# Reshaping the phase-F weight chunks of a hybrid RetNet / Mamba-2 layer: 8 k-blocks x 256 columns become 4 k-blocks x 512 columns

## What is computed

```
o_ret = (yr * silu(g_ret)) @ w_ret_o          # yr already times ret_gn_w; 2048 x 1024 weights
o_ssd = (ys_normed * ssd_norm_w) @ w_ssd_o    # 2048 x 1024 weights
g_r, g_s = split(gates)                       # gates = h @ w_in[:, 12352:14400]
out = (sigmoid(g_r) * o_ret + sigmoid(g_s) * o_ssd) @ w_out
x_new = x + gate * rmsnorm(out, norm_post)
```

## Time and profile before

| what | us |
|---|---|
| median of the two timed runs | 4121.48 |
| the two timed runs | 4078.60 and 4164.37 |
| the profiled execution | 4029.62 |
| its span on the slowest core, core 6 | 4027.9 |
| spans of the eight cores in it | 4001.4 to 4027.9 |

### The profile page before, as it was taken

One profiled execution on the slowest core, in us unless ns is written; L12 is line 12 of the kernel. 1 busy time (PEld: TensorE's weight loads), 2 busy tenths in 40 slices (PEclk: granted clock), 3 DMA queues, 4 the chain that ended last, 5 costly groups with the idle time before them and its releaser, 6 DMA issues.

```text
span 4027.9 us, 49014 instructions; the slowest of 8 cores (4001.4 to 4027.9 us)
## 1 busy us (share of the span) xinstructions
PE 2515.2 (62%) x15552; PEld 1579.3 (39%) x15552; DVE 1737.8 (43%) x2966; ACT 1341.8 (33%) x3063; POOL 515.8 (13%) x526
## 2 busy tenths in 40 slices
PE   7358679688688536556366363663646635394974
PEld 7335354263263325334153251532524424142431
DVE  0432524415425365564654646656466465010111
ACT  0233242341331325344263352543525435111121
POOL 0020120111201011010110111101101011303213
PEclk9579899899899757767577686776867767697997
DMA  4320110210200100101001000010000000414113
GB/s 134 105 76 17 52 56 6 65 38 11 80 11 17 54 6 6 37 1 33 10 1 42 1 26 17 1 43 1 22 21 1 27 1 28 150 63 146 63 56 133
DMA packets 143692, 166.85 MB, mean 41 GB/s; under 512 B 5072, under 2 KB 128464, under 8 KB 143312
## 3 DMA queue, kind: packets, MB, share of 16 engines
q1 hardware_dynamic: 138960, 146.94, 11.9%
q0 software_dynamic: 4480, 16.78, 1.1%
HBM read 138.54 MB, written 25.17 MB: 41 GB/s over the span
## 4 chain that ended last, share of the span: by engine, by line
PE 43%; DVE 24%; ACT 12%; issue 10%; DMA 5%; POOL 3%; DVEq 1%; ACTq 0%; SPq 0%; POOLq 0%
DVE s_acc L776 8%; PE ps_all L617 7%; PE ps_all L505 6%; PE ps_all L1047 6%; ACT s_Dec L913 5%; PE ps_all L899 4%; PE ps_all L741 3%; PE ps_all L600 3%; DVE s_S L858 3%; PE ps_all L1054 3%; PE ps_all L439 2%; PE ps_all L288 2%; PE ps_all L760 2%; DMA s_xF<-x 2%; PE ps_all L797 1%
## 5 line engine op out<-in xcount | busy, mean ns | idle before, releaser
L606 DVE TENSOR_TENSOR s_M<-ps_all,s_Th 128x512 bf16<-128x512 f32 x320 | 216.0, 689 | 438.9 <-PE ps_all L600 438.8
L913 ACT ACTIVATE s_Dec<-ps_all,s_nacum 128x128 f32<-128x128 f32 x1024 | 372.8, 366 | 96.0 <-PE ps_all L903 10.3
L856 PE MATMUL ps_all<-s_raw,s_B_tm 128*128 128x256 bf16 x272 | 98.5, 374 | 411.4 <-POOL s_raw L841 275.8
L617 PE MATMUL ps_all<-s_Vt,s_M 128*128 128x512 bf16 x1280 | 336.5, 391 | 27.4 <-DVE s_M L606 15.3
L899 PEld LDWEIGHTS ps_all<-s_ssdc,s_a 128*128 128x128 f32 x2048 | 339.7, 234 | 16.7
L776 DVE SCALAR_TENSOR_TENSOR s_acc<-s_raw,s_vecs,s_acc 128x2308 f32<-128x2308 f32 x128 | 335.6, 2622 | 14.0 <-DVE s_acc L776 0.9
L899 PE MATMUL ps_all<-s_ssdc,s_a 128*128 128x128 f32 x2048 | 337.3, 319 | 0.0
L1047 PE MATMUL ps_all<-s_yblk,s_wA 128*128 128x512 bf16 x1024 | 235.2, 383 | 133.3 <-DMA s_yblk<-yrT_scr 79.0
L760 PE MATMUL ps_all<-s_hT,s_wbfS 128*128 128x512 bf16 (+1 forms) x1216 | 277.3, 393 | 27.3 <-ACT s_wbfS L225 27.3
L505 PE MATMUL ps_all<-s_wbfR,s_hT 128*128 128x256 bf16 x2176 | 248.1, 277 | 44.8 <-ACT s_wbfR L225 29.5
L505 PEld LDWEIGHTS ps_all<-s_wbfR,s_hT 128*128 128x128 bf16 x2176 | 214.7, 99 | 78.3 <-issue 51.0
(11 more groups left out here) (155 smaller groups left out, 4267.4 us busy)
## 6 DMA issues: line engine op xcount, KB each, us to landing
s_wstR<-w_in SPq DMA_DIRECT2D x24, 1024.0 KB, 5.5
s_wstS<-w_in SPq DMA_DIRECT2D x32, 512.0 KB, 3.9
s_wst<-w_mod SPq DMA_DIRECT2D x12, 1024.0 KB, 5.2
s_dl<-dlt SPq DMA_DIRECT2D x32, 280.0 KB, 3.0
s_xt<-x SPq DMA_DIRECT2D x16, 512.0 KB, 3.7
yrT_scr<-s_yT POOLq DMA_DIRECT2D x16, 512.0 KB, 3.4
s_wstS<-w_in SPq DMA_DIRECT2D x8, 1024.0 KB, 5.2
ysT_scr<-s_ysT POOLq DMA_DIRECT2D x8, 1024.0 KB, 6.7
```

The costliest lines, as they stand in the source:

```text
L606: P.op("vector", lambda e, pss=pss, Mv=Mv, x0=x0: e.tensor_tensor(out=Mv[:], in0=pss[:], in1=Th[:, x0:x0 + 512], op=ALU.mult), reads=[pssb ...
L617: ins = e.matmul(psy[qt][:], lhsT=Mv[:, qt * 128:(qt + 1) * 128], rhs=Vt[:, kt, :], start=(ki == 0), stop=(ki == nk - 1))
L856: P.op("tensor", lambda e, d=d, t=t, bi=bi: e.matmul(bank(bi)[:, 0:256], lhsT=B_tm[:, t, :], rhs=xw_all[:, d, t, :], start=True, stop=True ...
L913: P.op("scalar", lambda e, Dec=Dec, d=d, r=r, q=q, t=t, sbk=sbk: e.activation(out=Dec[:, d, r, :], in_=bank(sbk[d])[:, r * 128:(r + 1) * 1 ...
```

## The change

`load_w` gets a parameter `nkc`, the number of k-blocks in a chunk. With the default, 8, it does what it did. In phase F it is called with 4 k-blocks and 512 columns. A chunk still has 1 MB and fills the same staging tile, which is viewed as 4 x 512 instead of 8 x 256. The pieces that a DMA reads in HBM become 2 KB instead of 1 KB. An A chunk is cast in four instructions of 128x512 instead of eight of 128x256. A branch has two column groups instead of four, and the order of its twelve chunks changes from A A G, four times, to A A A A G G, twice. `wAb` and `wGb` have two objects instead of four, one for each 512 columns.

```diff
-        def load_w(wst_ring, wbf_ring, src_view, c0, ncols, dst=None, dstbuf=None, scale_col=None, kc0=0, cast_eng="gpsimd"):
-            sv, sbuf_ = wst_ring.next()
-            P.dma("sync", lambda e: e.dma_start(out=sv[:, :, 0:ncols], in_=src_view[:, kc0:kc0 + 8, c0:c0 + ncols]),
-                  writes=[sbuf_])
+        def load_w(wst_ring, wbf_ring, src_view, c0, ncols, dst=None, dstbuf=None, scale_col=None, kc0=0, cast_eng="gpsimd", nkc=8):
+            sv_, sbuf_ = wst_ring.next()
+            if nkc == 8:
+                sv = sv_[:, :, 0:ncols]
+            else:
+                sv = sv_[:].rearrange("p a b -> p (a b)")[:, 0:nkc * ncols].rearrange("p (a b) -> p a b", a=nkc)
+            P.dma("sync", lambda e: e.dma_start(out=sv, in_=src_view[:, kc0:kc0 + nkc, c0:c0 + ncols]), writes=[sbuf_])
...
-                for kc in range(8):
+                for kc in range(nkc):
                     P.op("gpsimd", lambda e, kc=kc: e.tensor_scalar(
-                        out=bva[:, kc, :], in0=sv[:, kc, 0:ncols],
+                        out=bva[:, kc, :], in0=sv[:, kc, :],
...
-            wAb = [Buf("wA%d" % i) for i in range(4)]
-            wGb = [Buf("wG%d" % i) for i in range(4)]
+            wAb = [Buf("wA%d" % i) for i in range(2)]
+            wGb = [Buf("wG%d" % i) for i in range(2)]
...
-                for cu in range(4):
-                    for kh in range(2):
-                        load_w(wst_ring, None, src_o, cu * 256, 256, dst=wA[:, kh * 8:(kh + 1) * 8, cu * 256:(cu + 1) * 256], dstbuf=wAb[cu],
-                               scale_col=scol, kc0=kh * 8)
-                    load_w(wst_ring, None, w_in_v, 12352 + br * 1024 + cu * 256, 256, dst=wG[:, :, cu * 256:(cu + 1) * 256], dstbuf=wGb[cu],
-                           cast_eng="scalar")
+                for cu in range(2):
+                    for kq in range(4):
+                        load_w(wst_ring, None, src_o, cu * 512, 512, dst=wA[:, kq * 4:(kq + 1) * 4, cu * 512:(cu + 1) * 512], dstbuf=wAb[cu],
+                               scale_col=scol, kc0=kq * 4, nkc=4)
+                    for kq in range(2):
+                        load_w(wst_ring, None, w_in_v, 12352 + br * 1024 + cu * 512, 512, dst=wG[:, kq * 4:(kq + 1) * 4, cu * 512:(cu + 1) * 512],
+                               dstbuf=wGb[cu], kc0=kq * 4, nkc=4, cast_eng="scalar")
...
-                        P.op("tensor", mma, reads=[yblkb, wAb[fo // 2]], writes=[pab])
+                        P.op("tensor", mma, reads=[yblkb, wAb[fo // 4]], writes=[pab])
...
-                        P.op("tensor", mmg, reads=[wGb[fo // 2]], writes=[pgb])
+                        P.op("tensor", mmg, reads=[wGb[fo // 4]], writes=[pgb])
...
-            for cu in range(4):
-                load_w(wst_ring, None, src_o, cu * 256, 256, dst=wA[:, 0:8, cu * 256:(cu + 1) * 256], dstbuf=wAb[cu], cast_eng="scalar")
+            for cu in range(2):
+                for kq in range(2):
+                    load_w(wst_ring, None, src_o, cu * 512, 512, dst=wA[:, kq * 4:(kq + 1) * 4, cu * 512:(cu + 1) * 512], dstbuf=wAb[cu],
+                           kc0=kq * 4, nkc=4, cast_eng="scalar")
```

More of the change, by code:

```diff
@@ L224, in load_w @@
             if scale_col is None and cast_eng == "scalar":
-                P.op("scalar", lambda e: e.activation(out=bva, in_=sv[:, :, 0:ncols], func=AF.Copy),
-                     reads=[sbuf_], writes=[bbuf])
+                P.op("scalar", lambda e: e.activation(out=bva, in_=sv, func=AF.Copy), reads=[sbuf_], writes=[bbuf])
             elif scale_col is None:
-                P.op("gpsimd", lambda e: e.tensor_copy(out=bva, in_=sv[:, :, 0:ncols]),
-                     reads=[sbuf_], writes=[bbuf])
+                P.op("gpsimd", lambda e: e.tensor_copy(out=bva, in_=sv), reads=[sbuf_], writes=[bbuf])
             else:
-                for kc in range(8):
+                for kc in range(nkc):
                     P.op("gpsimd", lambda e, kc=kc: e.tensor_scalar(
-                        out=bva[:, kc, :], in0=sv[:, kc, 0:ncols],
+                        out=bva[:, kc, :], in0=sv[:, kc, :],
                         scalar1=vecs[:, scale_col + kc0 + kc:scale_col + kc0 + kc + 1], scalar2=0.0,
```

## The result

| | us |
|---|---|
| before, median of 26 runs | 4034.4 |
| changed, median of 28 runs | 4006.5 |
| ratio, 95% interval | 0.9926 (0.991 to 0.9942) |
| the same pair compared a second time | 0.9941 (0.9925 to 0.9958) |

The change made the kernel faster by 0.6 to 0.7%, some 24 to 30 us. That is under the 2% at which the prediction drew its line, so "same", to which it gave 0.93, is what came; but both intervals lie clear of 1, so the difference is real. I had forecast -16 us and a range of 4050 to 4150. The sign was right; the size was too small and the range missed.

The account below looks back on a forecast made before the run. TensorE's two load gaps in phase F bound the change: -4.5 (branch 0) and -11.1 (branch 1) sum to -15.6, say -16, from 4029.6 to 4013.6 profiled, or 4105 on the median's scale; range 4050 to 4150.

Parts of the forecast that it names:

- The range: Whole kernel: -16 us applied to the timed median 4121.5 gave 4105, with a range of 4050 to 4150.
- part 1: GpSimd's A casts: 128x512 takes 0.858 us, so a chunk's casts cost 4.10 us instead of 5.17.
- the slot chain: Phase F loads: two staging slots set when the last chunk is issued; model 57.8 us before, queue 57.4.
- P: Branch 1: the moment its first G cast ends, put at 3660.4, with four A chunks done instead of three.
- near 24 us after the first G cast: Sign for branch 1: issue of yblk near 24 us after the first G cast, against 36.3 before.
- casts scale better than I think: Rival on GpSimd's casts: 0.611 us for 128x512 gives -24; priced at -22, 4099; chance 0.17.
- Part 2, the transfers: Weight loads: 2 KB pieces instead of 1 KB, landing times kept; possible saving under 1 us in the sum.
- Part 3, branch 0: Slots in branch 0: the new order takes 51.1 us against 57.8; 6.0 after hand-overs, -4.5 after the yblk charge.
- The backlog ahead of yblk: Both branches: part of a G chunk is still in flight ahead of yblk, costing 1.5 us in each.
- Part 4, branch 1 and the cover: Branch 1: casts released 10.4 us later are covered with 2.1 us to spare; gain 12.6, net -11.1.
- Slower by exposed landings: Rival in both branches: seven exposed landings; 2.3 us more each cancels the gain, at 10.1 us 4138; chance 0.07.
- It does not do what it says: Rival on both branches: casts cost twice and A chunks land in 7.0 us; -3, 4118; chance 0.14.

Follow-up runs that it names:

- e4: Changed kernel with each A cast split in two of 128x256; ratio to the kernel before 0.9981.
- e2: Kernel before with only the chunk order changed to A A A A G G; ratio to the kernel before 0.9978.
- e5: Changed kernel with its G chunks read as 8 k-blocks x 256 columns again; ratio to the kernel before 0.9939.
- e1: Changed kernel profiled once more, no edit; ratio to the kernel before 0.9941.
- e6: Kernel before with its G chunks read as 4 k-blocks x 512 columns; ratio to the kernel before 1.0001.
- e11: Kernel before with only two objects instead of four for wA and wG; ratio to the kernel before 1.0004.

## Why the prediction was right or wrong

In short: two steps failed. The one that put the measured 4006.5 outside the range is the move of the forecast onto the two timed runs ("The range" below). The one that made the gain too small is the split of the cast's 481 ns by a memset (part 1). The waits and the path were right.

**What bounds the kernel, the two gaps, the slot chain: right.** Nothing moved outside the gaps, and the third stage is equal. The chain model gave 57.8 for the kernel before; for the changed one, with the measured 3.44 us for four casts in place of 4.10, it gives 21.6 + 7.0 + 17.2 + 2.0 = 47.8 in branch 0, and the mean over cores 4 to 7 from the first weight issue to `yblk` is 48.9 (58.5 before, over all cores). In branch 1 it gives 10.8 + 10.3 and the hand-overs, some 21.3, and 2.0 for the G cast that stands ahead of P; the mean from the first G cast to `yblk` is 25.0 (39.5 before). That is a gain of 14.5 where the text had 12.6. One of its signs was misread: it set "near 24 us after the first G cast" against "36.3 before", but both are counted from the end of that cast; from its start the rows give 38.4 before, and its sum would have been near 25 to 26.

**Part 1, the casts: the term that was mis-sized.** I split the 481 ns of the row by a memset of two columns, 104 ns fixed, and got 858 ns for 512. It is 692. On a straight line through the two widths the fixed part is 481 - 211 = 270 ns (an estimate from these two rows), not 104, and the step that failed is taking the fixed part of one instruction from another. A row of the kernel before that I had not used had the missing number, the same memset at 512 columns:

```profile
L848 POOL MEMSET s_S<- 128x512 f32 x8 | 4.1, 516 | 0.0
```

From 2 to 512 columns the memset grows by 516 - 104 = 412 ns, 0.81 ns for a column. Laid on top of the 481 ns, 256 more columns give 688, against 692 measured: the slope carried over from one instruction to the other, the fixed part did not. Eight exposed runs of four at 0.166 less are 5.3 us. The rival "casts scale better than I think", with its -22, was the one that came true; I had given it 0.17. Its price was near by luck in part: it rested on the cast row of 611 ns, which was not reached. The rule of the Trainium skill (GPSIMD Engine Reference, section Performance versus the Vector engine), 1.03 cycles for an element, which I had noted as neither confirmed nor excluded, would have given 0.70, an estimate; this case's rows, (692 - 481) / 256 = 0.82 ns for a column, are within 5% of its 0.86.

**Part 2, the transfers: right to leave at nothing.** e4 against e2, e5 against e1, and e6 against before are three comparisons of width at fixed order and fixed casts, and no stretch differs by more than 0.7 us in any of them, which is below what the ruler can tell.

**Part 3, branch 0.** The order itself is worth nothing there (79.7 in e2 and before); the text's 57.8 against 51.1 hides this, because it mixed the order with the casts. With C = 5.17 the same formula gives 56.5, 1.3 us better. That the casts carry branch 0 is what e4 shows.

**The backlog ahead of yblk: no cost shows.** I charged 1.5 us in each branch for a G chunk still in flight. It was in flight: on core 6 of e1 its cast starts at 3462.60, 1.9 us after `yblk` is issued. But from the `yblk` issue to the first sigmoid the mean is 20.9 in branch 0 (21.2 before) and 19.8 in branch 1 (20.3 before). So it got no longer; single cores scatter from 19.1 to 24.2 (before, in branch 0), so the 0.8 us by which the two means fell is not an effect that can be told. The charge of 3 us was the second term that was too high.

**Part 4, branch 1 and the cover: right.** -10.4 by the order, and the coarser objects cost nothing; e11 shows it by itself. The cover that I gave as 2.1 us was larger, in part since the casts were faster: on core 6 of e1 G0 went out 3642.29 - 3631.26 = 11.0 us ahead of its cast, where the text had 9.1.

**Sum.** -15.6, -5.3 for the casts, -3.0 for the backlog and -0.8 for what `yblk` gained instead gives -24.7; the gaps say -24.9, F says -24.9, the two ratios -24 and -30. By branch, the forecast had -4.5 and -11.1, and the gaps say -9.9 and -15.0. That the sum meets the gaps to 0.2 us is luck, as one stretch is known to 2 us at best. The gap between the two ratios, whose intervals meet at 0.9925 to 0.9942, is not explained by anything here.

**The range: the step that missed.** It missed for another reason than the mechanism. I moved the forecast from the profiled execution's 4029.6, where it gave 4013.6, to the median of the two runs, 92 us higher, and let the range start at 4050. The 26 runs show that those two were not the scale of this kernel: 17 of them lie at 4026 to 4037 and the other nine at 4078 and above. The eight spans of the profiled execution, 4001.4 to 4027.9, with mean clocks of 0.789 to 0.795, were the better anchor: by it the forecast, 4013.6, would have been 7 us from the measured 4006.5. Nor does a measurement of this kernel need 2% to tell a change: the interval of the ratio is 0.16% to either side.

**The rivals.** "Slower by exposed landings" had the right place: on core 6 the casts now do wait for transfers within a group, 0.6 to 2.9 us each time. It had the wrong price, as the median landings stayed at 5.7 to 6.5 us on core 6, below the 7.7 of its point of decision. (The longest landing of a chunk there, 12.3 us, stands right behind a `yblk` in the matmul stretch, and the kernel before has 12.5 at that place.) "It does not do what it says" did not come.

## What to carry to other kernels

When a load chain hangs on few slots, write down, for each order of chunks, which landings and which casts stay exposed, and do so with each engine's queue: the in-order engine that both casts and drains results decides how far the matmuls can run ahead. Price a wider instruction from its own row plus a slope, and take the slope from an instruction that the trace has at two widths; a fixed part taken from another instruction missed by 166 ns here. The most was not in reshaping the chunks (25 us) but in not putting the first operand that TensorE needs behind all of them, together with putting the casts of the later group behind the drains of the earlier (80 us in all, the 25 included).

## What the runs showed of the hardware that I had not expected

- A GpSimd multiply-and-cast of 128x256 takes 481 ns and of 128x512 692 ns, each followed by 0.17 us to the next that waits for it. The second 256 columns cost 0.82 ns each, as those of a memset do (0.81, from 104 ns at 2 columns and 516 at 512).
- Reading a 1 MB weight chunk in pieces of 2 KB instead of 1 KB changed no stretch of this kernel by more than 0.7 us (e4 against e2, e5 against e1, e6 against before).
- The same 2 MB transfer lands after 10.8 us on one core and 14.2 on another of the same execution, and on core 6 the median of the eight `w_in` chunks was 5.1, 5.5, 6.3, 6.5 and 7.0 us in five profiles (e11, e5, e6, e1, before). Why is left open; a difference of 3 us in one transfer of one core may not be read as an effect.
